# Later half gather and shorter router, reordered joint and last attention, products released by each turned column group

## The chip, the cores and the metric

The kernel runs on one core of a Trainium2 chip. The metric is the device time of one execution, in microseconds (us). The core's engines are TensorE (PE, matrix products and turns), VectorE (DVE), ScalarE (ACT), GpSimd (POOL) and SyncE (SP, which here only issues loads). Each engine runs its own instruction queue in order; semaphores tie the queues together, and 16 DMA engines move data. Everything is float32.

## The reference

One token block of 256 latent rows and two contexts of 256 rows, width 1024, goes through three layers. `first_block` is gated linear attention and a mixture of experts; `second_block` is a joint attention layer (latent attention with 8 heads and grouped attention with 8 heads over context and latent keys) and a last layer (windowed attention and a short convolution).

```python
# experts
scores = sigmoid(h @ w_router); sel = scores + b_router
# the best group of 4 of 16 experts by the sum of its best two, then its best two experts
out += gates[:, e] * ((silu(h @ w1[e]) * (h @ w3[e])) @ w2[e])      # every e
# joint layer
q, k, v = heads_ab(adaln(x, mod) @ w_in)                            # also for the context
x = x + gate * ((attention over [context, latent] * silu(g)) @ w_out)
xc = xc + gate_c * ((attention over context * silu(gc)) @ w_out)
# last layer
oc = window attention with sink; od = gb * short_conv(gcv * gh, conv_w)
x = x + gate * ((concat[oc, od] * silu(g)) @ w_out)
```

## The kernel before, in words

Each engine has one block of code, and the order of the calls in it is the order of its queue. There is no planner: all orders are written by hand, and the same list of steps stands in the blocks of PE, ACT and DVE.

**Banks.** `Banks` hands the eight accumulator banks out in turn. `open` makes PE wait until the eighth-last bank was evicted, `filled` tells the reader that it may evict, `wait` is that reader's wait.

**Turns and products.** `turn(use, src)` transposes normed rows with PE, eight column groups k into eight banks. ACT evicts the even groups (L1190), DVE the odd ones (L1706), with the modulation applied. `wait_turned(use)` then holds PE until all eight are there, and `project` (L562) or `project_T` (L574) runs eight products, one per k. Uses 0, 1, 3, 4 and 5 turn the first norm, the router's input, the latent rows of the joint layer, and the context and latent rows of the last layer.

**Router and gather.** The logits come from 16 small products on the turned rows (L746). DVE ranks the experts with linked small operations (L1882 to L1940): `places` (five operations) is called for each of the two token tiles, twice. PE counts tokens ahead (five products, L758 to L762), DVE makes the selection matrix `sel` (L1928, L1929), and PE gathers the tokens into expert order as products with `sel`, in two parts of 32 products (L771), which ACT (L1332) and DVE (L1944) evict.

**Experts.** 16 experts, one after another: GpSimd copies (`stage`, L2271) the 64 rows of an expert, PE runs `up` (32 products, L787), ACT takes Silu (L1377), DVE the product (L1974), PE turns it (L793), ACT copies it (L1379), PE runs `down` (16 products, L800). An expert with more than 64 tokens repeats this behind a branch. SP loads three pieces of 2 MB per expert into seven slots, in a fixed order (L1105); a slot of an `up` piece is free when that `up` is done, a `down` slot when that `down` is done. ACT and DVE run a hardware loop over eight pairs of experts.

**Joint layer.** Projections per tile, then queries and keys (L562, L899), grouped and latent norms on DVE that ask ACT for reciprocal roots (`head_rstd`, L1420 to L1423), turns of the heads (L908, L922), products for the gates (L849), then attention in 32 iterations of two units: turns of probabilities (L949), values (L958), scores three iterations ahead (L939). `ab_between` puts the modulation products of later layers (L530) between. `gate(u)` spreads a gate row over all partitions: DVE makes a diagonal (L1713), PE two products of four steps (L593), ACT two copies. Gates 2 and 3 come after the attention, then the eight output products (L562).

**Last layer.** Keys, values, queries, attention gates, output gates in two halves (`cdga`, L574), turns (L1051, L1055), then eight iterations of attention with twelve chunks of the convolution's input products (L574, two after each of the first six iterations), then the output.

## Time and profile before

| what | value |
| --- | --- |
| median of 3 runs | 1092.01 us (1090.19 to 1094.64) |
| the profiled execution, its own time | 1090.92 us |
| its span, first to last instruction | 1089.2 us |
| busy in the span | PE 969.7 us (89%), DVE 369.5 (34%), ACT 292.0 (27%), POOL 27.8 (3%) |
| mean granted TensorE clock | 0.969 of full |
| DMA traffic | 217.62 MB, mean 200 GB/s |

A busy PE is not PE at its peak, and a share over the whole span mixes stages with different limits. The rows below are read stage by stage: the instruction, when it started, how long it ran, and in brackets how long its engine had been idle before it and what released it.

### The profile page before, as it was taken

Reading aid. Unit: us, or ns where it says so; the run is one execution under the profiler, and the core shown is the slowest. Engines: PE = TensorE matmul, PEld = TensorE weight load, DVE = VectorE, ACT = ScalarE, POOL = GpSimd, SP = SyncE. Lnnn points to the kernel's source line nnn. Section 1 sums busy time; section 2 is a strip of 40 time slices with the busy share of each in tenths; the row PEclk is TensorE's granted clock in tenths of the full one; section 3 lists DMA queues with packets and bytes.
Section 4 is the critical chain, followed back from the end, with each engine's and each line's share of the span. In section 5 each row is a group of like instructions: output and inputs, shape, how many; then the busy total and the mean of one; then the engine's idle time right before and its main releaser. Section 6 shows DMA issues by size and latency. Waiting matters only on the chain.

```text
span 1089.2 us, 12096 instructions
## 1 busy us (share of the span) xinstructions
PE 969.7 (89%) x4358; PEld 518.8 (48%) x4359; DVE 369.5 (34%) x878; ACT 292.0 (27%) x678; POOL 27.8 (3%) x48
## 2 busy tenths in 40 slices
PE   3899989999878877688779999979999899997998
PEld 1464446554463322233225665557455445575763
DVE  1100597614540000000002231277667323246442
ACT  3210544233210000000001321356666211215320
POOL 0100200000000000000001000000000000000000
PEclk8999999999979989999989999989999999998999
DMA  9964565593597999989998202104644104332321
GB/s 352 320 230 156 103 232 194 177 335 106 193 348 287 398 395 397 397 339 398 394 397 301 78 1 78 68 1 155 225 139 102 40 0 149 102 136 78 94 62 39
DMA packets 99364, 217.62 MB, mean 200 GB/s; under 512 B 2853, under 2 KB 5209, under 8 KB 99177
## 3 DMA queue, kind: packets, MB, share of 16 engines
q1 hardware_dynamic: 94480, 206.45, 52.7%
q0 software_dynamic: 1696, 5.72, 2.1%
q10 hardware_dynamic: 3128, 4.62, 1.1%
q8 instruction: 42, 0.69, 0.3%
q14 instruction: 18, 0.14, 0.0%
HBM read 211.27 MB, written 5.51 MB: 199 GB/s over the span
## 4 chain that ended last, share of the span: by engine, by line
PE 74%; DMA 9%; DVE 6%; ACT 5%; issue 3%; SPq 2%; POOLq 0%; ACTq 0%; DVEq 0%; POOL 0%
PE bank L562 27%; PE bank L787 9%; PE bank L574 9%; DMA arena<-in_w_gate_e_dram 4%; PE bank L854 4%; PE bank L939 3%; PE bank L800 3%; PE bank L958 3%; DMA arena<-in_w_mod_dram 3%; PE bank L530 3%; PE bank L949 3%; DMA arena<-in_w_up_e_dram 2%; PE bank L771 2%; SPq L1105 1%; PE bank L849 1%
## 5 line engine op out<-in xcount | busy, mean ns | idle before, releaser
L562 PE MATMUL bank<-arena 128*128 128x512 f32 (+3 forms) x768 | 305.7, 556 | 4.0 <-ACT arena L1190 2.0
L562 PEld LDWEIGHTS bank<-arena 128*128 128x128 f32 x768 | 144.1, 190 | 153.6 <-issue 140.2
L787 PE MATMUL bank<-arena 128*64 128x512 f32 x544 | 130.8, 636 | 23.2 <-issue 23.2
L574 PE MATMUL bank<-arena 128*128 128x256 f32 (+1 forms) x384 | 99.3, 418 | 2.9 <-ACT arena L1539 1.5
L787 PEld LDWEIGHTS bank<-arena 128*64 128x64 f32 x544 | 46.2, 147 | 105.9 <-issue 105.9
L574 PEld LDWEIGHTS bank<-arena 128*128 128x128 f32 x384 | 72.5, 191 | 31.2 <-issue 21.7
L800 PE MATMUL bank<-arena 128*64 128x512 f32 x272 | 63.8, 610 | 9.6 <-ACT arena L1379 9.0
L1377 ACT ACTIVATE arena<-bank 128x256 f32<-128x256 f32 x16 | 6.1, 383 | 199.4 <-PE bank L787 199.4
L530 PE MATMUL bank<-arena,silu_c 128*32 128x512 f32 x384 | 50.2, 648 | 5.3 <-DMA arena<-in_w_mod_dram 2.9
L1974 DVE TENSOR_TENSOR arena<-arena,bank 128x256 f32<-128x256 f32 x16 | 6.7, 421 | 138.3 <-ACT arena L1377 138.3
L939 PE MATMUL bank<-arena 64*128 64x512 f32 (+3 forms) x160 | 49.6, 574 | 4.5 <-ACT arena L1636 2.3
L1539 ACT ACTIVATE arena<-bank,small 128x512 f32<-128x512 f32 (+1 forms) x80 | 47.9, 616 | 0.5
L1550 ACT ACTIVATE arena<-bank 128x512 f32<-128x512 f32 (+1 forms) x80 | 37.4, 516 | 20.0 <-PE bank L949 19.0
L949 PE MATMUL bank<-con,arena 128*128 128x128 f32 x256 | 37.8, 279 | 5.3 <-DVE arena L2139 3.4
L854 PE MATMUL bank<-arena 128*64 128x256 f32 x384 | 42.1, 380 | 0.0
L800 PEld LDWEIGHTS bank<-arena 128*64 128x64 f32 x272 | 21.9, 139 | 40.5 <-issue 40.5
L1723 DVE TENSOR_TENSOR arena<-bank,gate_rows 128x512 f32<-128x512 f32 x16 | 11.1, 692 | 88.4 <-PE bank L562 79.7
L949 PEld LDWEIGHTS bank<-con,arena 128*128 128x128 f32 x256 | 28.7, 141 | 22.4 <-DVE arena L2139 13.9
L2119 DVE TENSOR_REDUCE small<-bank 128x1 f32<-128x256 f32 (+1 forms) x64 | 33.9, 554 | 14.9 <-PE bank L939 14.4
L1977 DVE TENSOR_TENSOR gate_rows<-bank,gate_rows 128x512 f32<-128x512 f32 x16 | 11.1, 692 | 78.5 <-PE bank L800 78.5
L2139 DVE TENSOR_SCALAR arena<-arena,small 128x512 f32<-128x512 f32 (+1 forms) x80 | 34.7, 433 | 2.8
L854 PEld LDWEIGHTS bank<-arena 128*64 128x64 f32 x384 | 27.3, 137 | 15.7 <-issue 2.3
(327 smaller groups left out, 956.2 us busy)
## 6 DMA issues: line engine op xcount, KB each, us to landing
arena<-in_w_up_e_dram SPq DMA_DIRECT2D x16, 2048.0 KB, 20.3
arena<-in_w_gate_e_dram SPq DMA_DIRECT2D x16, 2048.0 KB, 20.0
arena<-in_w_down_e_dram SPq DMA_DIRECT2D x16, 2048.0 KB, 20.2
arena<-in_w_mod_dram SPq DMA_DIRECT2D x12, 2048.0 KB, 12.2
arena<-in_mod_w_dram SPq DMA_DIRECT2D x12, 2048.0 KB, 8.1
arena<-in_gla_w_in_dram SPq DMA_DIRECT2D x6, 2048.0 KB, 11.4
arena<-in_cd_w_in_dram SPq DMA_DIRECT2D x6, 2048.0 KB, 7.9
arena<-in_ab_w_in_dram SPq DMA_DIRECT2D x5, 2048.0 KB, 8.0
```

Of the source, the lines that this page charges most:

```text
L530: mm = pe.matmul(ps[32 * j:32 * j + 32, :], silu_c[:, blk, k, :], w[:, k, :], start=(k < 4), stop=(k >= 4), tile_position=(0, 32 * j))
L562: mm = pe.matmul(ps[:, 0:n], lhs[:, k, tile * P:(tile + 1) * P], w[:, k, c0:c0 + n], start=(k == 0), stop=(k == kd_ - 1))
L574: mm = pe.matmul(ps[:, i * n:(i + 1) * n], w[:, k, c * P:(c + 1) * P], rhs[:, k, 0:n], start=(k == 0), stop=(k == KC - 1))
L787: mm = pe.matmul(up_b[64 * j:64 * j + 64, :], h[:, k, :], blocks[:, g + n:u + n + 1:u - g, :], start=(k == 0), stop=(k == KC - 1), tile_po ...
L800: mm = pe.matmul(dn_b[64 * q:64 * q + 64, :], ffT[:, kc % 2, 64 * (kc // 2):64 * (kc // 2) + 64], w2[:, kc, 512 * q:512 * q + 512], start= ...
L854: mm = pe.matmul(ps[GD * v:GD * v + GD, n * T:(n + 1) * T], w[:, k, at:at + GD], rhs[:, k, 0:T], start=(k == 0), stop=(k == KC - 1), tile_ ...
L939: mm = pe.matmul(ps[:, 0:(hi - lo) * P], q, k, start=True, stop=True)
L949: mm = pe.transpose(ps[:, i * P:(i + 1) * P], prob[u % 4][:, i * P:(i + 1) * P], ident)
L1539: act.activation(prob[u % 4][:, 0:(hi - lo) * P], ps[:, 0:(hi - lo) * P], ACT.Exp, bias=per_unit(at_max, u), accum_out=per_unit(at_den, u) ...
L1550: act.activation(probT[g % 2][:, j, 0:hi - lo, P * (t % 2):P * (t % 2) + P], ps[:, 0:(hi - lo) * P].rearrange("p (k t) -> p k t", t=P), AC ...
L2119: dve.tensor_reduce(per_unit(at_max, u), ps[:, 0:(hi - lo) * P], AX.X, ALU.max, negate=True)\
L2139: dve.tensor_scalar(p, p, rden, None, ALU.mult).then_inc(p_scaled, 1)
```

## The change

Banks are handed out from a list, so that three can be held by the experts while the others turn over. `wait_turned` takes a column group and stands in the product's loop. The router ranks both tiles in one call, counts with two products, and writes `sel` part by part. The gather's second part stands behind expert 0's `up` on PE, and ahead of expert 0's Silu and product on ACT and DVE. ACT's and DVE's loops over experts are written out. GpSimd's handling of extra tokens stands behind the next copy; for expert 0 it stands ahead of expert 1's copy. In the joint layer two calls of `grouped_rstd` move ahead on ACT, gates 2 and 3 go into iterations 16 and 20, the flush to 28, and the first output product to 30; the wait for the last mixed groups stands before the fifth output product. In the last layer the second half of the output gates follows the turns of the keys, ACT's table load follows it, and one chunk of the convolution stands before the first iteration. Buffers move to constants that are no longer read.

```diff
     def open(self, pe, name, sem, value):
-        n = len(self.freed)
-        if n >= 8:
-            pe.wait_ge(*self.freed[n - 8])
-        self.freed.append((sem, value))
-        self.at[name] = n
-        return self.banks[n % 8]
+        n = self.order.pop(0)
+        if self.freed[n] is not None:
+            pe.wait_ge(*self.freed[n])
+        self.freed[n] = (sem, value)
+        self.used[n] += 1
+        self.at[name] = (n, self.used[n])
+        self.order.append(n)
+        return self.banks[n]
+
+    def hold(self, names):
+        self.held = [self.at[x][0] for x in names]
+        self.order = [n for n in self.order if n not in self.held]
+
+    def give_back(self):
+        self.order += self.held
 
...
-        act1, act2 = view(10240, 256), view(10496, 256)
-        ffT = view(10752, 2, P)
+        spent = con[:, cols["levels"][0]:cols["levels"][0] + 768]
+        act1, act2, ffT = spent[:, 0:256], spent[:, 256:512], spent[:, 512:768].rearrange("p (c s) -> p c s", c=2)
         y_buf = [gate_rows[:, 0, 0:512], gate_rows[:, 0, 512:1024]]
-        y_x, hs_x = view(11008, 512), view(SPARE + SLOT, KC, CAP)
+        y_x, hs_x = iota, gate_rows[:, 1, 512:1024].rearrange("p (k s) -> p k s", k=KC)
...
+        AB_GATE_AT, AB_OUT_AT = [16, 20], [30]
         CONV_CHUNKS = [(w, c) for w in ("cd3", "cd4", "cd2") for c in range(4)]
+        CONV_AT = [[0], [1, 2], [3, 4], [5, 6], [7, 8], [9, 10], [11], [], []]
...
-            def wait_turned(use):
-                pe.wait_ge(turned_a, 4 * TURN_AT[use] + 4)
-                pe.wait_ge(turned_v, 4 * TURN_AT[use] + 4)
-
-            def project(name, wname, c0, n, tile, lhs, sem_, value):
+            def wait_turned(use, k):
+
+                pe.wait_ge((turned_a, turned_v)[k % 2], 4 * TURN_AT[use] + k // 2 + 1)
+
+            def project(name, wname, c0, n, tile, lhs, sem_, value, turned=None):
...
                 for k in range(kd_):
+                    if turned is not None:
+                        wait_turned(turned, k)
                     mm = pe.matmul(ps[:, 0:n], lhs[:, k, tile * P:(tile + 1) * P], w[:, k, c0:c0 + n],
...
+                        if turned is not None and i == 0:
+                            wait_turned(turned, k)
...
             turn(0, xn)
-            wait_turned(0)
             for h in range(HG):
-                project_T(f"k{h}", "k", [h], 512, hT, k_ready, h + 1)
+                project_T(f"k{h}", "k", [h], 512, hT, k_ready, h + 1, turned=0 if h == 0 else None)
...
-            wait_turned(1)
             pe.wait_ge(route_in, 16)
             ps = banks.open(pe, "parts", parts_copied, 4)
             for k in range(KC):
                 j = k % 4
+                wait_turned(1, k)
                 mm = pe.matmul(ps[32 * j:32 * j + NE, 0:T], w_route[:, k, :], h2T[:, k, :],
...
             mask = small[:, 96:128].rearrange("p (t e) -> p t e", t=TT)
             ps = banks.open(pe, "ranks", ranked, 1)
-            pe.matmul(ps[:, 0:NE], before, mask[:, 0, :], start=True, stop=True)
-            pe.matmul(ps[:, NE:2 * NE], ones, mask[:, 0, :], start=True, stop=False)
-            pe.matmul(ps[:, NE:2 * NE], before, mask[:, 1, :], start=False, stop=True)
-            pe.matmul(ps[:, 2 * NE:3 * NE], ones, mask[:, 0, :], start=True, stop=False)
-            mm = pe.matmul(ps[:, 2 * NE:3 * NE], ones, mask[:, 1, :], start=False, stop=True)
+            both = mask.rearrange("p t e -> p (t e)")
+            pe.matmul(ps[:, 0:TT * NE], before, both, start=True, stop=True)
+            mm = pe.matmul(ps[:, TT * NE:2 * TT * NE], ones, both, start=True, stop=True)
...
-            pe.wait_ge(sel_ready, TT)
-            for part in range(2):
+            def gather(part):
+                pe.wait_ge(sel_ready, TT * (part + 1))
...
+            gather(0)
+
 
             moe = [banks.open(pe, f"moe{i}", experts_done, 1) for i in range(3)]
             up_b, t_b, dn_b = moe
+            banks.hold([f"moe{i}" for i in range(3)])
...
                 up(hs[e % 2], e, up_done)
+                if e == 0:
+                    gather(1)
                 pe.wait_ge(ff_ready, e + 1)
                 turn_ff(ff_turned)
...
-                wait_turned(use)
                 lhs, off = (hT_ctx, 2) if use == 2 else (hT_lat, 0)
                 for t in order:
-                    project(f"c{t}", "ab0", 0, 512, t - off, lhs, c_ready, AB_AT[t] + 1)
+                    project(f"c{t}", "ab0", 0, 512, t - off, lhs, c_ready, AB_AT[t] + 1,
+                            turned=use if t == order[0] else None)
...
-                if m == 30:
+                if m in AB_GATE_AT:
+                    gate(2 + AB_GATE_AT.index(m))
+                if m == 28:
                     mod_flush()
+                if m in AB_OUT_AT:
+                    pe.wait_ge(mixed, NG // 2)
+                    out_rows(AB_OUT_AT.index(m))
+
+            def out_rows(n):
+                t, c = ABY[n]
+                project(f"aby{c}{t}", f"abo{c}", 0, 512, t, mixT4, y_added, 4 + n + 1)
...
-            gate(2)
-            gate(3)
-            pe.wait_ge(mixed, NG)
             def keys_and_values(t):
-                project(f"cdkv{t}", "cd1", 0, 256, t, hT, cdkv_ready, CD_AT[t] + 1)
-
-            for n, (t, c) in enumerate(ABY):
-                project(f"aby{c}{t}", f"abo{c}", 0, 512, t, mixT4, y_added, 4 + n + 1)
+                project(f"cdkv{t}", "cd1", 0, 256, t, hT, cdkv_ready, CD_AT[t] + 1,
+                        turned=4 if t == 2 else 5 if t == 0 else None)
+
+            for n in range(len(AB_OUT_AT), len(ABY)):
+                if n == 4:
+                    pe.wait_ge(mixed, NG)
+                out_rows(n)
                 if n == 5:
                     turn(4, view(HIGH, 4, D))
-            wait_turned(4)
             for t in (2, 3):
                 keys_and_values(t)
             turn(5, view(HIGH, 4, D))
-            wait_turned(5)
...
-            for g in range(2):
-                project_T(f"cdga{g}", "cd6", [2 * g, 2 * g + 1], T, hT, cdga_ready, g + 1)
+            project_T("cdga0", "cd6", [0, 1], T, hT, cdga_ready, 1)
...
                 mm = pe.transpose(ps[:, t * P:(t + 1) * P], ckv_sb[:, t, 0:P], ident)
             banks.filled("wkT", mm)
+            project_T("cdga1", "cd6", [2, 3], T, hT, cdga_ready, 2)
             pe.wait_ge(gqkT_ready, 11)
...
             def cd_between(m):
-                for n in (2 * m, 2 * m + 1):
-                    if n < len(CONV_CHUNKS):
-                        w, c = CONV_CHUNKS[n]
-                        project_T(f"conv{n}", w, [c], T, hT, conv_in, n + 1)
+                for n in CONV_AT[m + 1]:
+                    w, c = CONV_CHUNKS[n]
+                    project_T(f"conv{n}", w, [c], T, hT, conv_in, n + 1)
 
             begin, run = attention(CD_GROUPS, NU, cd_probT, cd_scores, cd_values, lambda n: None, cd_between)
             begin()
+            cd_between(-1)
             run()
...
+            flags = extra_flag[0:1, :, :].rearrange("p e t -> p (e t)")
+            for e in range(NE):
+                i, b = e // 2, e % 2
+                act.wait_ge(hs_ready, e + 1)
+                slot0 = slot_of(act, e * (1 + EXTRA))
+                any_extra = act.value_load(flags[:, e * EXTRA:e * EXTRA + 1], min_val=0, max_val=1)
...
+                if e == 0:
+                    gather(1)
+                act.wait_ge(up_done, e + 1)
+                act.activation(act1, up_b[:, 0:256], ACT.Silu).then_inc(silu_done, 1)
...
+                if m in AB_GATE_AT:
+                    gate(2 + AB_GATE_AT.index(m))
 
             begin, run = attention(AB_GROUPS, 0, ab_probT, ab_between, False)
+            grouped_rstd(2)
             queries(0)
             keys_values(0)
-            grouped_rstd(2)
             queries(1)
...
             queries(2)
+            grouped_rstd(3)
             keys_values(2)
-            grouped_rstd(3)
...
-            gate(2)
-            gate(3)
...
-            for g in range(2):
+            def out_gates(g):
...
-            act.preload_act_table_set(LN_EXP)
+
+            out_gates(0)
             for t in range(TT):
                 ps = banks.wait(act, f"wqT{t}")
                 act.activation(qwT[:, :, t * P:(t + 1) * P], ps[:, :].rearrange("p (g t) -> p g t", g=4), ACT.Copy)\
                    .then_inc(gqkT_ready, 1)
             ps = banks.wait(act, "wkT")
             act.activation(kwT[:, :], ps[:, :], ACT.Copy).then_inc(gqkT_ready, 1)
+            out_gates(1)
+            act.preload_act_table_set(LN_EXP)
...
-            for t in range(TT):
-                places(place[:, t, :], pick[:, t, :], GROUPS, EPG)
+            places(place.rearrange("p t e -> p (t e)"), pick.rearrange("p t e -> p (t e)"), TT * GROUPS, EPG)
             link(dve.tensor_scalar(mask, place, 2.0, None, ALU.is_lt))
             link(dve.tensor_tensor(tmp32, pick, mask, ALU.mult))
             link(dve.tensor_reduce(gscore.rearrange("p t g -> p (t g)"),
                                    tmp32.rearrange("p t (g e) -> p (t g) e", e=EPG), AX.X, ALU.add))
-            for t in range(TT):
-                places(gplace[:, t, :], gscore[:, t, :], 1, GROUPS)
+            places(gplace.rearrange("p t g -> p (t g)"), gscore.rearrange("p t g -> p (t g)"), TT, GROUPS)
...
-            dve.tensor_copy(cnt, ps[:, 2 * NE:3 * NE])
-            dve.tensor_copy(rank, ps[:, 0:2 * NE].rearrange("p (t e) -> p t e", t=TT)).then_inc(ranked, 1)
+            ahead, all_ = (ps[:, i * TT * NE:(i + 1) * TT * NE].rearrange("p (t e) -> p t e", t=TT) for i in range(2))
+            dve.tensor_copy(rank, all_)
+            link(dve.tensor_copy(slot_v, ahead))
+            link(dve.tensor_tensor(cnt, rank[:, 0, :], rank[:, 1, :], ALU.add))
+            dve.tensor_tensor(slot_v[:, 1, :], slot_v[:, 1, :], rank[:, 0, :], ALU.add).then_inc(ranked, 1)
             dve.wait_ge(ranked, 1)
             link(dve.tensor_tensor_scan(slot0, ones[:, 0:NE], cnt, 0.0, ALU.mult, ALU.add))
             link(dve.tensor_tensor(slot0, slot0, cnt, ALU.subtract))
-            link(dve.tensor_tensor(slot_v, rank, outer(slot0, TT), ALU.add))
...
-            for t in range(TT):
-                link(dve.tensor_scalar(sel[:, t, :], iota, slots_ab[:, t, 0:1], None, ALU.is_equal))
-                dve.scalar_tensor_tensor(sel[:, t, :], iota, slots_ab[:, t, 1:2], sel[:, t, :], ALU.is_equal, ALU.add)\
-                   .then_inc(sel_ready, 1)
+            for part in range(2):
+                for t in range(TT):
+                    places_in, row = iota[:, T * part:T * part + T], sel[:, t, T * part:T * part + T]
+                    link(dve.tensor_scalar(row, places_in, slots_ab[:, t, 0:1], None, ALU.is_equal))
+                    dve.scalar_tensor_tensor(row, places_in, slots_ab[:, t, 1:2], row, ALU.is_equal, ALU.add)\
+                       .then_inc(sel_ready, 1)
...
-            for part in range(2):
+            def gather(part):
                 for k in range(1, KC, 2):
                     ps = banks.wait(dve, f"gath{part}{k}")
                     dve.tensor_scalar(hg[:, k, T * part:T * part + T], ps[:, 0:T], coef[:, 2, 0, k:k + 1],
                                       coef[:, 2, 1, k:k + 1], ALU.mult, ALU.add).then_inc(hg_v, 1)
-            up_b, t_b, dn_b = [banks.banks[banks.at[f"moe{i}"] % 8] for i in range(3)]
+
+            gather(0)
+            up_b, t_b, dn_b = [banks.banks[banks.at[f"moe{i}"][0]] for i in range(3)]
             dve.wait_ge(gate_bc, 4)
 
...
-                if m == 30:
+                if m + 1 in AB_GATE_AT:
+                    gate(2 + AB_GATE_AT.index(m + 1), mod2[:, 0, 16:24, AB_GATE_AT.index(m + 1)])
+                if m == 28:
                     mod_col(23)
...
-            gate(2, mod2[:, 0, 16:24, 0])
-            gate(3, mod2[:, 0, 16:24, 1])
...
             stage(0, 0)
+            stage_extra(0)
             pool.wait_ge(hg_a, KC)
             pool.wait_ge(hg_v, KC)
             stage(1, 1)
...
             with pool.Fori(0, NE // 2 - 1) as i:
                 for b in range(2):
                     e = i * 2 + b
-                    stage_extra(e)
                     pool.wait_ge(up_done, e + 1)
                     stage(e + 2, b)
-            stage_extra(NE - 2)
-            pool.wait_ge(up_done, NE - 1)
+                    stage_extra(e + 1)
             stage_extra(NE - 1)
...
```

## Rows read from the trace of the kernel before

**Rows 1.** The page: GB/s of 40 slices, and the ended-last chain by engine.

```profile
GB/s 352 320 230 156 103 232 194 177 335 106 193 348 287 398 395 397 397 339 398 394 397 301 78 1 78 68 1 155 225 139 102 40 0 149 102 136 78 94 62 39
...
PE 74%; DMA 9%; DVE 6%; ACT 5%; issue 3%; SPq 2%; POOLq 0%; ACTq 0%; DVEq 0%; POOL 0%
```

**Rows 2.** Chain in order of time: start us, us, what.

```profile
372.99 20.42 DMA arena<-in_w_up_e_dram
```

**Rows 3.** Timeline, router: start us, us, engine, line, instruction [idle before <-releaser].

```profile
292.84 1.06 PE L746 MATMUL bank<-arena,w_route 128*16 128x256 f32 x16 [1.42 <-ACT arena L1190]
...
297.02 0.22 DVE L1892 TENSOR_TENSOR small<-small 128x64 f32<-128x64 f32 x1
...
302.32 0.61 PE L758 MATMUL bank<-small,con 128*128 128x16 f32 x2 [4.20 <-DVE small L1908]
...
304.74 0.17 DVE L1915 COPY small<-bank 128x16 f32<-128x16 f32 x1 [1.60 <-PE bank L762]
...
306.56 0.49 DVE L1928 TENSOR_SCALAR arena<-con,small 128x512 f32<-128x512 f32 x1
```

**Rows 4.** Timeline, gather, expert 0 and expert 1's down.

```profile
309.07 17.09 PE L771 MATMUL bank<-arena 128*128 128x256 f32 x64 [4.44 <-DVE arena L1929]
...
319.30 0.54 DVE L1944 TENSOR_SCALAR arena<-bank,coef 128x256 f32<-128x256 f32 x1 [1.18 <-PE bank L771]
...
320.91 0.61 POOL L2271 COPY arena<-arena 128x512 f32 x1 [18.06 <-ACT arena L1332]
...
326.09 7.09 PE L787 MATMUL bank<-arena 128*64 128x512 f32 x32
...
335.57 5.35 PE L800 MATMUL bank<-arena 128*64 128x512 f32 x16 [0.56 <-ACT arena L1379]
...
349.80 3.65 PE L800 MATMUL bank<-arena 128*64 128x512 f32 x16 [0.56 <-ACT arena L1379]
```

**Rows 5.** Windows: stretch, busy us per engine, granted clock, DMA share, GB/s.

```profile
324.00:326.00 2.00, 2.00 (x11) 1.55 (x9) 0.54 (x1) 0.82 (x3) 0.00 (x0) 1.00 0.08 29
...
334.00:336.00 2.00, 0.87 (x4) 0.46 (x6) 0.42 (x1) 0.38 (x1) 0.61 (x1) 0.92 0.76 161
...
336.00:338.00 2.00, 2.00 (x6) 0.59 (x4) 0.00 (x0) 0.00 (x0) 0.00 (x0) 0.50 1.03 372
```

**Rows 6.** Timeline, first products behind turns 0, 3 and 5.

```profile
38.93 13.99 PE L574 MATMUL bank<-arena 128*128 128x512 f32 x32 [1.36 <-ACT arena L1190]
...
645.30 13.97 PE L562 MATMUL bank<-arena 128*128 128x512 f32 x32 [0.83 <-ACT arena L1190]
...
928.95 3.26 PE L562 MATMUL bank<-arena 128*128 128x256 f32 x14 [1.16 <-ACT arena L1190]
```

**Rows 7.** Timeline, heads of the joint attention.

```profile
703.39 0.69 DVE L2031 TENSOR_TENSOR mod_rows<-arena,rstd 128x512 f32<-128x512 f32 x1 [9.04 <-ACT rstd L1423]
...
714.65 3.55 PE L922 MATMUL bank<-con,arena 128*96 128x128 f32 x16 [5.76 <-DVE arena L2102]
...
725.83 0.69 DVE L2031 TENSOR_TENSOR mod_rows<-arena,rstd 128x512 f32<-128x512 f32 x1 [3.37 <-ACT rstd L1423]
...
745.63 1.91 PE L922 MATMUL bank<-con,arena 128*96 128x128 f32 x16
```

**Rows 8.** Timeline, end of the joint attention.

```profile
853.36 1.95 PE L958 MATMUL bank<-arena,gate_rows 128*64 128x256 f32 x16 [0.74 <-ACT arena L1550]
...
856.96 1.98 PE L593 MATMUL bank<-gate_diag,con 128*128 128x512 f32 x4 [1.66 <-DVE gate_diag L1713]
...
862.09 18.19 PE L562 MATMUL bank<-arena 128*128 128x512 f32 x42
```

**Rows 9.** Timeline, start of the last attention.

```profile
983.09 4.43 PE L939 MATMUL bank<-arena 64*128 64x512 f32 x12 [2.26 <-ACT arena L1636]
...
990.01 1.71 PE L949 MATMUL bank<-con,arena 128*128 128x128 f32 x8 [2.49 <-DVE arena L2139]
```

**Rows 10.** Waits of PE, experts: engine, line, releaser: us in total, times, longest.

```profile
PE bank L787 <- issue: 23.2, 9, 3.8
```

167 lines of the change are left out of this document (82 added, 85 removed).

## The prediction

> **What bounds the kernel now.** Read the page's shares of the chain that ended last first, then the GB/s of its 40 slices: TensorE (PE) carries 74% of the chain and DMA 9%, and for eight of nine slices in the middle the traffic stands at 394 to 398 GB/s [rows 1]. So there are two regimes. Outside the experts a piece of PE time, or PE idle that is not itself a wait for a load, is worth its length. Inside the experts the chain runs through expert weights, for example 20.42 us on one load [rows 2]; there only what brings the first buffers back earlier counts. Then read the timeline at each edited place for the idle ahead of the first PE instruction and its releaser.
>
> **Products behind a turning wait (turns 0, 3 and 5).** PE waited 1.36, 0.83 and 1.16 us for the last of eight turned column groups [rows 6]. Now group k releases only product k, and ScalarE and VectorE finish the eight groups in pairs. Turn 0: PE is free at 38.93 - 1.36 = 37.57, where about four groups are ready, and a product of 32/4 = 8 steps takes 13.99/4 = 3.5 us, so it ends at 41.1 instead of 42.4: 1.3 us. Its bounds are 0 (the weights of k may land only then; no row shows it) and 1.36. Turn 3: the same arithmetic gives 0.8. Turn 5: eight 256-column steps take about 1.8 us (3.26 us for 14, [rows 6]), and the last group ends them at one step after 928.9; 929.1 instead of 930.7 is 1.5, bounds 0.5 and 1.6. What waits behind these waits on PE is only the same product, so a wait costs nothing else.
>
> **Router.** The logits' first product waited 1.42 us for turn 1 and took 1.06 [rows 3]; run along with the evictions it ends one step after the last: 0.9 us less. From the first ranking comparison at 297.02 to the first rank product at 302.32 VectorE runs 25 linked operations, 0.21 us each [rows 3]. Batching both tiles removes 10 (2.1), doubled widths of the ten left cost back some 0.4 in all: 1.7. Five rank products become two; they took from 302.32 to the copy at 304.74, about 0.43 each, so 1.3 less, and two more linked operations behind them give 0.4 back. The first selection now writes half the width: 306.56 to the gather's start at 309.07 is 2.5 us; full and half price of the elements bound it by 2.5 and 1.25, I take 1.7, so 0.8. Together 3.4, with turn 1 about 4.2 us.
>
> **Gather in halves.** The whole gather is 64 products in 17.09 us. Its first half ended about 319.2 (its last eviction starts at 319.30), GpSimd copied expert 0's rows at 320.91 for 0.61, and up(0) could not start before 326.09 because the second half stood in PE's queue [rows 4]. Now up(0) starts 0.1 after the copy, at 321.6: 4.5 earlier, and with the router 8.7 earlier, 317.4. It ends at t0 = 324.5. But the second half (about 6.9 us at full clock: 326.1 - 319.2) is now between up(0) and down(0), and the 2.4 us chain of Silu, product, turn, copy (333.18 to 335.57, [rows 4]) is mostly still open behind it, since ScalarE and VectorE first evict the half.
>
> What does that do to the loads? DMA had nothing from about 324 (29 GB/s in 324:326) until the first returned buffers, issued at 333.2, moved data from about 334.5 [rows 5]; a 2.1 MB load at 395 GB/s [rows 1] takes 5.3 us. Before: two loads by up(0) fill 334.5 to 345.1, the third is released by down(0) at 335.57 + 5.35 = 340.9, the next two by up(1) 7 us later, and the queue is never empty; five loads are through at 361.0. After: two loads fill t0+1.3 to t0+11.9; down(0) ends at t0 + 6.9 + 2.3 + 3.65 = t0+12.9 (3.65 is down(1) at full clock, [rows 4]), so the third load moves only from t0+14.2 to t0+19.5, and the two by up(1) from t0+21.1 to t0+31.7 = 356.2. The loads are 4.8 us ahead of 361.0: of 8.7 us earlier start, 3.9 are given back in two new holes. One price more: the clock. In the 2.4 us gap before down(0) the granted clock fell to its 1.2 GHz level (0.92 in 334:336, 0.50 in 336:338), and down(0) took 5.35 instead of 3.65 [rows 4, 5]. The new gap ahead of up(0) is as long and has no matrix work in it at all; I charge 1.7 once. Experts: 4.8 - 1.7 = 3.1 us. Bounds: both gaps slow and PE's half of the gather late, -1; no fall, +4.8. The loads carry this shift to the end of the experts, since from 373 on PE waits for them by far more [rows 2].
>
> The Trainium skill (TensorE: Matmul & The Clock Gate, Part 4: PE-mode transpose) says that transposes don't count as busy for that clock. The drop in a gap that contained two transposes agrees with it; by that rule the gap after the second half, which has only transposes in it, would cost another 1.7, and the total below would be 1069.4.
>
> **Unrolled loops, banks, other queues.** ScalarE's and VectorE's loop over pairs of experts goes; its registers and branches lay beside up (7.09 us): 0, but see D. Three banks are held from the first half on, so the second half turns over five; each is evicted 0.5 us after it is filled: 0. GpSimd stages expert 1 about 2.3 us after the second half ends, wanted 5.8 after: 0. SP's load of cd2 now waits for the moved gate half, 1.7 us later, and is used more than 20 us after it lands: 0.
>
> **Heads of the joint attention.** VectorE idled 9.04 us until 703.39 and 3.37 until 725.83 for reciprocal roots whose sums were ready: ScalarE had queries and keys ahead of them in its queue [rows 7]. Moved ahead, the first three small activations (0.8 us) run while ScalarE had waited anyway; VectorE's grouped norm then runs from 697.2 to 702.5, inside the old idle, and the latent norm starts at 702.8 (the copies it needs end there) rather than 708.7. Its result reaches PE at 709.5, not 714.65, behind PE's own work until 708.9: of 5.76 us idle 0.6 stay, and the 16 transposes take 1.9 as the later ones (745.63) instead of 3.55 [rows 7]. That is 5.1 + 1.6 = 6.7. Next late would be the second latent norm, wanted at 717.4 and due at 715.4, then nothing: 14 us of gate products follow and PE reaches the transposes of 745.63 at 738.9. Bounds 3 (ScalarE's order makes the second norm late) and 7.
>
> **Joint attention.** Its last values ended at 853.36 + 1.95 = 855.3 and the output products began at 862.09: 6.8 us of two gate rounds on the path [rows 8]. They go into iterations 16 and 20, where PE is busy almost without a hole, so their products stay as a cost: 2 x 1.98 = 4.0 [rows 8]. VectorE's diagonal and ScalarE's copies lie under PE there, bounds 0 and 1.5 more. The first output product moves forward ahead of the last turns, and the three others stand in front of the wait for the last mixed group, which covers it. The small flush moves by two iterations at no price. 6.8 - 4.0 = 2.8; take 2.9 for half-filled holes, bounds 1 and 3.5.
>
> **Last attention.** Before: PE waited 2.26 us for the evicted keys, ran the first scores in 4.43 us, waited 2.49, and at the slow clock its next steps were long too [rows 9]. The second half of the output gates (7 us) now stands between the turns and the scores and covers the 2.26, paid back by nothing since it only moves; the first conv chunk (3.5) stands in the 2.49. At full clock the three scores take 3.3, and turns, scores and convs after them lose about 2 us of slowness. 2.3 + 1.1 + 2.5 + 2.0 = 7.9, less 1.0 for what ScalarE evicts later (the gate half and its table load now run beside the first scores): 6.9. The tail keeps its waits, as only one chunk stands in iteration 5 but two iterations of exponentials are done by then. Bounds 3 and 8.
>
> **Sum.** 1.3 + 3.1 + 0.8 + 6.7 + 2.9 + 1.5 + 6.9 = 23.2 us off the profiled execution's own 1090.92 (span 1089.2 and 1.7 around it): 1067.7. The median of the runs shown is 1.1 above that execution, which would give 1068.8. Forecast 1068.
>
> **The rivals.**
> *A, queues, not PE, hold the two reordered stages.* For: ScalarE and VectorE have in-order chains there and the estimates leave 2 us. Against: in the trace both idle for PE. Heads 3, last attention 3: 1068 + 7.6 = 1076. Chance 0.2.
> *B, the early up(0) gives the experts nothing:* the holes at the third and fourth load eat it, with two slow gaps: 1068 + 4 = 1072. For: 3.9 us of it are already in my sum. Chance 0.12.
> *C, the change doesn't do what it says at the turns:* weights or the second evicting engine arrive last. 1068 + 1.3 + 0.9 + 0.8 + 1.5 = 1072.5. Chance 0.06.
> *D, slower: code.* Straight code for 16 experts is fetched anew for each on ScalarE and VectorE while the queues are full. PE, straight already, shows 23.2 us in 9 waits put down to issue, up to 3.8 [rows 10], though those hold waits for loads as well. If each engine lost 3 us between up and down of each expert, 6.0 against the 3.8 that PE waits at most would be 2.2 x 16 = 35 us more: 1103. It decides from 5.3 us per expert on (3.8 + 24/16). Against: the code after a wait has 7 us of up to arrive. Chance 0.04.
> The Trainium skill (Runtime: NRT & Kernel Launch, Instruction fetch mechanics) gives D its reason: fetching ahead is sequential, and a taken branch out of its window has to fetch first; every expert skips the body for extra tokens. No run here shows such a fetch on these two engines.
> *Forecast:* 0.58, its own range 1063 to 1073.
>
> **Range and chances.** 1061 to 1079 holds the forecast, A, B and C. What a measurement of this kernel can tell from no change is about 0.5%, 5.5 us. Faster 0.94, same 0.02, slower 0.04.
>
> **What would show it.** Right: PE idle before the first latent transposes under 1 us; gates inside the attention and no hole between the last values and output product 4 of over 1 us; scores of the last attention released by PE's own queue, not ScalarE; up(0) starting some 9 us earlier relative to the transposes of turn 1; a DMA hole of 2 us after the second returned load; total traffic rate unchanged behind it. Wrong: expert 15's last product ending later than about 574 (before 577.8, less 1.3 and 3.1), idle on PE named after ScalarE in the heads, gate rounds costing over 2 us each, or Silu starting later than 0.5 us behind up.

## The result and the profile after

The changed kernel takes 1066.45 us (median of 4 runs, 1066.13 to 1070.58), the kernel before 1093.33 us (4 runs, 1090.19 to 1097.04). The ratio is 0.9762 with a 95% interval of 0.9736 to 0.9788. The forecast was 1068 us. The profiled execution took 1066.23 us with a span of 1064.5, against 1090.92 and 1089.2 before: 24.7 us, where the sum said 23.2.

From the page of the changed kernel, the lines that answer to [rows 1]:

```profile
GB/s 352 335 235 160 79 263 158 182 301 188 96 395 339 400 394 398 394 339 394 397 396 352 128 1 79 70 1 158 165 153 146 14 40 82 156 159 79 116 44 39
...
PE 77%; DMA 9%; DVE 5%; ACT 3%; issue 2%; SPq 2%; POOLq 1%; ACTq 0%; POOL 0%; DVEq 0%
```

The rate in the middle is the old one, 394 to 400 GB/s but for two slices at 339 (before: 394 to 398, with one such slice among eight). On PE 15.1 us of idle time went, and 9.6 us of busy time (969.7 to 960.1), as less of it ran at the slow clock (mean granted clock 0.978, before 0.969); the other engines' share of the chain fell, so PE's rose. Laid out by stage, with the same instruction as the mark in both chains of waits:

| stage, mark at its end | before, us | after, us | gain | predicted |
|---|---|---|---|---|
| start to the norm after the first attention's output | 284.02 | 284.12 | -0.1 | 1.3 |
| router and experts, to the first product of the joint layer | 294.39 | 288.87 | 5.5 | 3.1 |
| to the first product behind turn 3 | 66.89 | 66.07 | 0.8 | 0.8 |
| heads, to iteration 2's first scores | 114.65 | 107.36 | 7.3 | 6.7 |
| joint attention, to the second output product | 109.02 | 106.59 | 2.4 | 2.9 |
| turns 4 and 5, to the gates of the last layer | 80.86 | 79.51 | 1.4 | 1.5 |
| last attention, to its first output product | 107.65 | 100.27 | 7.4 | 6.9 |

**Turn 0.** The timeline of PE at the second pair of value products, and windows of the same place (columns as in [rows 5]):

```profile
110.17 15.70 PE L578 MATMUL bank<-arena 128*128 128x512 f32 x32
```

```profile
110.00:112.00 2.00, 2.00 (x5) 0.96 (x4) 2.00 (x4) 0.00 (x0) 1.42 (x2) 0.65 0.00 0
112.00:114.00 2.00, 2.00 (x3) 0.66 (x2) 1.06 (x2) 1.57 (x1) 2.00 (x5) 0.50 0.59 96
```

The products that came 1.45 us earlier (37.48 in the chain, against 38.93 in [rows 6]) were followed by a pair that took 15.7 us instead of 14.0, with PE busy all the time and its granted clock at 0.50, the 1.2 GHz level. Before it, PE had run 3.7 us of products with 16 rows. The profile of the kernel before shows no fall there.

**Router, gather, expert 0.** The timeline that answers to [rows 3, 4]:

```profile
291.46 2.04 PE L763 MATMUL bank<-arena,w_route 128*16 128x256 f32 x16
...
296.42 0.29 DVE L1927 TENSOR_TENSOR small<-small 128x128 f32<-128x128 f32 x1
...
300.03 0.64 PE L776 MATMUL bank<-small,con 128*128 128x32 f32 x2 [3.22 <-DVE small L1941]
...
303.44 0.35 DVE L1966 TENSOR_SCALAR arena<-con,small 128x256 f32<-128x256 f32 x1
...
305.16 8.85 PE L786 MATMUL bank<-arena 128*128 128x256 f32 x32 [4.07 <-DVE arena L1967]
...
315.67 0.61 POOL L2311 COPY arena<-arena 128x512 f32 x1 [15.11 <-issue]
...
316.33 7.09 PE L805 MATMUL bank<-arena 128*64 128x512 f32 x32 [2.33 <-POOL arena L2311]
...
323.35 7.17 PE L786 MATMUL bank<-arena 128*128 128x256 f32 x32
```

The wait for turn 1 is gone, the ranking takes 3.6 us (296.42 to 300.03) where it took 5.3, and the gather starts at 305.16 instead of 309.07. up(0) comes 9.8 us earlier, at full clock, after a gap of 2.33 us. Down(0) runs at 332.49 in 3.65 us, not in the 5.35 of [rows 4]. Of the two holes that the prediction laid out in the loads, the first shows as two windows at half the rate; windows of 1 us, GB/s last:

```profile
336.00:337.00 1.00, 1.00 (x8) 0.47 (x6) 0.69 (x1) 0.00 (x0) 0.00 (x0) 1.00 1.06 410
337.00:338.00 1.00, 1.00 (x7) 0.34 (x4) 0.00 (x0) 0.00 (x0) 0.00 (x0) 1.00 0.82 176
338.00:339.00 1.00, 1.00 (x8) 0.39 (x6) 0.00 (x0) 0.00 (x0) 0.00 (x0) 1.00 0.57 195
```

The second, expected near 344, is no hole: the windows from 339 to 343 moved 293 to 338 GB/s, those of 343 to 345 over 400 and the next 305.

**Later stages.** Timelines of the changed kernel's PE against [rows 7 to 9]: the first latent transposes and the two gate rounds inside the joint attention; then the product behind the last values, the last attention's first scores and the step behind the convolution chunk.

```profile
702.77 1.95 PE L943 MATMUL bank<-con,arena 128*96 128x128 f32 x16 [0.37 <-DVE arena L2142]
...
787.96 1.88 PE L611 MATMUL bank<-gate_diag,con 128*128 128x512 f32 x4
...
807.09 1.88 PE L611 MATMUL bank<-gate_diag,con 128*128 128x512 f32 x4
...
852.94 9.28 PE L578 MATMUL bank<-arena 128*128 128x512 f32 x21
...
963.45 2.85 PE L960 MATMUL bank<-arena 64*128 64x512 f32 x12
966.23 3.72 PE L592 MATMUL bank<-arena 128*128 128x256 f32 x16
970.37 1.44 PE L970 MATMUL bank<-con,arena 128*128 128x128 f32 x8 [0.42 <-DVE arena L2179]
```

A wait of 5.76 us became 0.37, the output products start on the heels of the last values, the waits of 2.26 and 2.49 us became none and 0.42, and the slow clock of [rows 9] (three scores in 4.43 us, now 2.85) did not come.

### The profile page after: what moved, and what is told of

It reads as the page before. It is cut to its first block, busy times and chain, and to the rows that moved or that the text cites. A ratio compares the mean times of both kernels' runs of the same rounds, so it can differ in the third digit from the quotient of the medians.

```text
span 1064.5 us, 11944 instructions
## 1 busy us (share of the span) xinstructions
PE 960.1 (90%) x4352; PEld 513.7 (48%) x4353; DVE 368.5 (35%) x874; ACT 291.8 (27%) x678; POOL 27.8 (3%) x48
## 4 chain that ended last, share of the span: by engine, by line
PE 77%; DMA 9%; DVE 5%; ACT 3%; issue 2%; SPq 2%; POOLq 1%; ACTq 0%; POOL 0%; DVEq 0%
PE bank L578 27%; PE bank L805 9%; PE bank L592 9%; DMA arena<-in_w_up_e_dram 4%; PE bank L875 4%; PE bank L818 3%; PE bank L960 3%; PE bank L979 3%; PE bank L544 3%; PE bank L870 3%; PE bank L970 3%; DMA arena<-in_w_gate_e_dram 2%; DMA arena<-in_w_mod_dram 2%; SPq L1133 2%; PE bank L786 2%
## 5 line engine op out<-in xcount | busy, mean ns | idle before, releaser
L578 PEld LDWEIGHTS bank<-arena 128*128 128x128 f32 x768 | 144.4, 191 | 152.0 <-issue 140.8
L805 PE MATMUL bank<-arena 128*64 128x512 f32 x512 | 122.0, 631 | 22.6 <-issue 20.3
L805 PEld LDWEIGHTS bank<-arena 128*64 128x64 f32 x512 | 43.8, 145 | 98.9 <-issue 96.1
L818 PE MATMUL bank<-arena,con 128*64 128x512 f32 x272 | 62.1, 597 | 9.6 <-ACT con L1409 9.0
L1407 ACT ACTIVATE con<-bank 128x256 f32<-128x256 f32 x16 | 6.1, 383 | 191.3 <-PE bank L805 191.3
L2014 DVE TENSOR_TENSOR con<-con,bank 128x256 f32<-128x256 f32 x16 | 6.7, 421 | 131.1 <-ACT con L1407 131.1
L960 PE MATMUL bank<-arena 64*128 64x512 f32 (+3 forms) x160 | 47.1, 540 | 2.2 <-ACT arena L1569 2.2
L818 PEld LDWEIGHTS bank<-arena,con 128*64 128x64 f32 x272 | 21.5, 136 | 39.3 <-issue 39.3
L875 PEld LDWEIGHTS bank<-arena 128*64 128x64 f32 x384 | 27.3, 137 | 15.7 <-issue 2.3
L1758 DVE TENSOR_TENSOR arena<-bank,gate_rows 128x512 f32<-128x512 f32 x12 | 8.3, 692 | 63.5 <-PE bank L578 63.5
```

Of the source, the lines that this page charges most:

```text
L578: mm = pe.matmul(ps[:, 0:n], lhs[:, k, tile * P:(tile + 1) * P], w[:, k, c0:c0 + n], start=(k == 0), stop=(k == kd_ - 1))
L805: mm = pe.matmul(up_b[64 * j:64 * j + 64, :], h[:, k, :], blocks[:, g + n:u + n + 1:u - g, :], start=(k == 0), stop=(k == KC - 1), tile_po ...
L818: mm = pe.matmul(dn_b[64 * q:64 * q + 64, :], ffT[:, kc % 2, 64 * (kc // 2):64 * (kc // 2) + 64], w2[:, kc, 512 * q:512 * q + 512], start= ...
L875: mm = pe.matmul(ps[GD * v:GD * v + GD, n * T:(n + 1) * T], w[:, k, at:at + GD], rhs[:, k, 0:T], start=(k == 0), stop=(k == KC - 1), tile_ ...
L960: mm = pe.matmul(ps[:, 0:(hi - lo) * P], q, k, start=True, stop=True)
```

## The experiments

Each time is a median; each ratio is to the kernel before, run on the same chip. The times of one kernel differ by up to 10 us from one execution to the next, so the verdicts on parts rest on the stages of the traces, the ratios beside them.

**1. Turn 0 alone.** Kernel before, with:

```diff
-            wait_turned(0)
+                        if turned is not None and i == 0:
+                            pe.wait_ge((turned_a, turned_v)[k % 2], 4 * TURN_AT[turned] + k // 2 + 1)
```

> Kernel before with one edit: the first key product waits for each turned column group by itself. In the changed kernel the products started 1.45 us earlier, but the second pair of value products (110.2 to 125.9) took 15.7 us instead of 14.0 with a granted clock of 0.65 and 0.50 between 110 and 114, where the kernel before had 1.00, although PE never stood idle. Theory (clock): the same fall comes again, since nothing ahead of it differs from the changed kernel; value product 3 ends at 125.8 to 125.9, the stage is not shorter, and the whole time is that of before within 0.5 us. Rival (something else held PE there, such as an eviction that the other parts of the change moved): no fall, value product 3 ends at 124.3, and the whole is 1.3 to 1.5 us faster by the trace's span.

Measured: 1091.63 against 1092.35 us, ratio 0.9983 (0.9963 to 1.0003). The fall came again (0.83, 0.50 and 0.81 in the three windows from 110 to 116). That looked like the theory, but runs 2 and 3, whose text up to there is that of the kernel before, have it too. Windows of run 2, with turn 0 as it was:

```profile
110.00:112.00 2.00, 2.00 (x11) 0.72 (x8) 2.00 (x5) 0.00 (x0) 0.00 (x0) 0.92 0.00 0
112.00:114.00 2.00, 2.00 (x3) 0.97 (x4) 2.00 (x5) 0.00 (x0) 1.79 (x3) 0.50 0.10 12
```

So the fall is not caused by the change, and the reason given in the expectation was wrong: the same text ahead of the place doesn't decide whether it comes. Run 9 put this to the test.

**2. Heads alone.** Kernel before, with ScalarE's order:

```diff
+            grouped_rstd(2)
             queries(0)
             keys_values(0)
-            grouped_rstd(2)
@@
             queries(2)
+            grouped_rstd(3)
             keys_values(2)
-            grouped_rstd(3)
```

> Kernel before with one edit: ScalarE takes the reciprocal roots of the grouped queries ahead of the queries and keys that stood in its queue. Theory: this alone gives what the heads' stage gained in the changed kernel, 7.3 us (first latent transpose 5.1 us earlier and at full clock, no granted clock of 0.5 around 712): ratio 0.9933, span 1082. The trace must show VectorE's waits of 9.04 and 3.37 us gone. Rival (the stage gained because PE arrived in it in another state, or from the banks' new order): under 3 us, ratio 0.997 or more.

Measured: 1084.00 us, ratio 0.9914 (0.9886 to 0.9942), which holds 0.9933. In the profile the first latent transposes have lost their wait, exactly as in the changed kernel:

```profile
710.36 1.95 PE L922 MATMUL bank<-con,arena 128*96 128x128 f32 x16 [0.38 <-DVE arena L2102]
```

The stage itself is 3.9 us shorter in this execution, the slowest of the five (1088.57), not 7: a fall came at 750 to 757 instead of the old one at 710 to 716.

**3. Joint attention alone.** Kernel before, with:

```diff
+                if m in AB_GATE_AT:
+                    gate(2 + AB_GATE_AT.index(m))
+                if m in AB_OUT_AT:
+                    pe.wait_ge(mixed, NG // 2)
+                    out_rows(AB_OUT_AT.index(m))
@@
-            gate(2)
-            gate(3)
-            pe.wait_ge(mixed, NG)
```

> Kernel before with the joint attention's part alone: the two rows of gates are built in iterations 16 and 20, the first output product runs in iteration 30, the small flush in iteration 28. Theory: 2.4 us, as in the changed kernel (6.8 us of gate rounds leave the path, some 3.5 to 4 us of their products and the longer iterations stay): ratio 0.9978. Rival (the gates' products fall into holes that PE had there anyway): 6 us, ratio 0.9945. A second rival (exponentials are late by the two gates' copies on ScalarE): nothing, ratio 1.000.

Measured: 1089.63 us, ratio 0.9974 (0.9952 to 0.9995). From the start of modulation product 18 to the last layer's gates it needs 186.01 us against 188.72: 2.7. The theory holds, both rivals fall.

**4. Last attention alone.** Kernel before, with the split output gates and one convolution chunk ahead of the first iteration (the rest of the change's part as it stands in the diff):

```diff
+            project_T("cdga1", "cd6", [2, 3], T, hT, cdga_ready, 2)
             pe.wait_ge(gqkT_ready, 11)
@@
             begin()
+            cd_between(-1)
             run()
```

> Kernel before with the last attention's part alone: second half of the output gates behind the turns, one convolution chunk ahead of the first iteration, table load behind both. Theory: the 7.4 us of the changed kernel come from here alone: ratio 0.9932, and no granted clock under 1.00 between 980 and 1000. Rival (half of it came from the earlier arrival of turns 4 and 5 and of the joint attention's evictions): 3 to 4 us, ratio 0.9965.

Measured: 1083.86 us, ratio 0.9908 (0.9874 to 0.9941). From the gates to the first output product 100.45 us, before 107.82, changed kernel 100.44. No clock under 1.00 in the stage. All of it comes from here.

**5 and 6. Both halves first, and that with loops.** Changed kernel, with

```diff
             gather(0)
+            gather(1)
@@
                 up(hs[e % 2], e, up_done)
-                if e == 0:
-                    gather(1)
```

and the same on ScalarE and VectorE; in 6 these two run their loop over eight pairs again.

> Changed kernel with one part undone: both halves of the gather run ahead of up(0) again; the shorter router and everything else stay. Theory (two holes in the loads): starting up(0) some 4.5 us earlier is given back almost whole, because the third load waits for down(0), which stands behind the second half, and the fourth and fifth wait for up(1); so undoing it costs only about 0.6 to 1.2 us from the last gate rows before the router to the end of expert 15. Rival (the early up(0) is worth its length): 4 to 4.5 us more, whole kernel 0.4% slower than the changed one.

> As both_halves_first, and ScalarE and VectorE run their loop over eight pairs of experts as in the kernel before, in place of straight code for 16 experts. Theory (code is free, as the instructions between two experts have 7 us of up to arrive): expert stage equal to both_halves_first within 0.3 us. Rival D (straight code is fetched anew for every expert): with loops the stage is shorter by 1 us or more, and Silu starts sooner behind up than with straight code.

Measured: 1070.48 us, ratio 0.9794 (0.9743 to 0.9846), and 1070.75 us, 0.9792 (0.9738 to 0.9845). From turn 1's last group of transposes to the start of expert 15's down it takes 279.18 and 279.42 us; in the changed kernel 279.58. The early up(0) is worth nothing that these profiles show, and they speak against the rival's 4 us. They don't exclude it: the distance varies from 278.2 to 284.0 us over four profiles of the changed kernel's text (run 10), run 5's profiled execution was the fastest of its five (1064.87), and the whole times, 0.9794 and 0.9792 against 0.9762, lie 0.3% higher (against run 9's 0.9778 0.15%), where the rival named 0.4%, within intervals of half a per cent either way. Straight code costs nothing that shows: 0.24 us between 5 and 6, the same wait of 1.02 us between up(0) and the turn behind it in both, and PE's waits in the experts no longer with it than with loops. Waits of PE in the stage, changed kernel first, loops second (as [rows 10]; run 5: 22.5 us in 8 waits):

```profile
PE bank L805 <- issue: 23.1, 9, 4.1
```

```profile
PE bank L806 <- issue: 26.3, 10, 4.4
```

**7. Whole waits.** Changed kernel, where the first product behind each turn waits for groups 7 and 8 (`if k == 0: wait_turned(turned, 6); wait_turned(turned, 7)`).

> Changed kernel with the turning waits whole again (turns 0, 1, 3, 4 and 5: the first product waits for all eight column groups). Theory: turn 0 1.4, the router's first product 0.9, turn 3 0.8 and turn 5 1.4 us come back, in all 4.5 us of PE time, of which turn 0's part can hide under a fall of the granted clock at 110: 3.1 to 4.5 us over the changed kernel, ratio to before 0.979 to 0.981. Rival (the order of the first products' steps doesn't matter, since the evictions end when they end and PE only waits inside the product): under 1 us.

Measured: 1071.57 us, ratio 0.9799 (0.9748 to 0.9851). The waits are back, at turns 0, 1, 3 and 5:

```profile
39.41 2.81 PE L594 MATMUL bank<-arena 128*128 128x512 f32 x6 [1.57 <-ACT arena L1222]
...
293.39 1.06 PE L767 MATMUL bank<-arena,w_route 128*16 128x256 f32 x16 [1.46 <-DVE arena L1744]
...
642.84 3.67 PE L579 MATMUL bank<-arena 128*128 128x512 f32 x8 [0.88 <-DVE arena L1744]
...
916.77 18.73 PE L579 MATMUL bank<-arena 128*128 128x256 f32 x59 [0.85 <-DVE arena L1744]
```

Their sum is 4.76 us, and the profiled execution (1071.37) is 5.1 us over the changed kernel's, in which turn 0's gain was lost to the clock while here up(0) ran with a fall. The mechanism is shown; its total only within such falls.

**8. No chunk ahead.** Changed kernel with `CONV_AT = [[], [0, 1], [2, 3], [4, 5], [6, 7], [8, 9], [10, 11], [], []]`.

> Changed kernel with the last attention's convolution chunks one iteration later: none ahead of the first iteration, two in each of the next six; the split output gates stay. Theory: the chunk ahead of the first iteration covered the wait of 2.49 us for the exponentials (and kept the clock up), so the last attention takes 2 to 3.5 us more than in the changed kernel. Rival (the gate half alone did it): within 0.5 us of the changed kernel.

Measured: 1075.09 us, ratio 0.983 (0.9779 to 0.9881). The stage takes 105.27 us, 4.8 more than in the changed kernel; the wait is back, and behind it a granted clock of 0.50 in 972:974:

```profile
971.03 1.90 PE L970 MATMUL bank<-con,arena 128*128 128x128 f32 x8 [4.07 <-DVE arena L2179]
```

The theory's sign is right, its 2 to 3.5 us too low. Of the 7.4 us the one chunk ahead of the first iteration carries 4.8; the other 2.6 are, by difference, the gate half's.

**9. The changed kernel once more.**

> The changed kernel once more, unedited, beside its own variants. Theory (the falls of the granted clock are drawn anew in each execution and not set by the kernel's text): the stage times without a fall repeat within 0.1 us (heads 107.3, last attention 100.4, turn 3 and turn 5 as before), while the falls at 110, around 320, at 405 to 460 and at 742 come at other places or not at all, and shift the end by 1.5 to 3 us. Rival (they belong to the kernel): the profile repeats with a fall at 110 to 114 and none before up(0) or at 742. Ratio to before 0.976 in either case.

Measured: 1067.07 us, ratio 0.9778 (0.9754 to 0.9801). The profile is another one. The value products and a window that had 0.50:

```profile
110.19 14.00 PE L578 MATMUL bank<-arena 128*128 128x512 f32 x32
```

```profile
112.00:114.00 2.00, 2.00 (x6) 0.95 (x5) 1.07 (x2) 1.55 (x1) 2.00 (x5) 1.00 0.59 92
```

Turn 0's lead is kept this time: turn 1's last transposes start at 287.46, against 289.27 in the first profile and 289.17 before. Instead up(0) ran slowly behind its 2.33 us gap:

```profile
316.00:318.00 2.00, 2.00 (x6) 0.48 (x4) 0.00 (x0) 0.00 (x0) 0.00 (x0) 0.52 1.02 386
318.00:320.00 2.00, 2.00 (x8) 0.62 (x6) 0.00 (x0) 0.00 (x0) 0.00 (x0) 0.62 1.05 387
```

It took 8.78 us for 7.09, the 1.7 that the prediction charged; the gather's first half, behind a wait of 4.06 us, came back to full clock later and took 10.08 us for 8.85; and the heads had a fall at 742 to 747 (1.5 us). The theory holds for these places, and the last attention repeats to 0.01 us (100.44). It doesn't hold for all: the four ups between 404 and 465, each behind a wait of 2 to 3.3 us, took 8.5 to 8.8 us in both profiles. Over all 14 profiles of this study the fall near 110 came 7 times, in kernels with either form of turn 0.

**10. Direct up(0).** Changed kernel, with

```diff
-                pe.wait_ge(hs_ready, e + 1)
-                up(hs[e % 2], e, up_done)
                 if e == 0:
+                    up(hg[:, :, 0:CAP], e, up_done, direct=True)
                     gather(1)
+                else:
+                    pe.wait_ge(hs_ready, e + 1)
+                    up(hs[e % 2], e, up_done)
@@
-            stage(0, 0)
+            pool.sem_inc(hs_ready, 1)
```

> Changed kernel; expert 0's first rows begin at place 0 always, so up(0) reads the gathered columns where they lie, each step released by the eviction of its column group, and GpSimd's copy for expert 0 is gone. Theory (loads wait for the buffers that up(0), down(0) and up(1) return, and all three move with up(0)): the wait of 2.33 us before up(0) goes, up(0) starts 2.2 us earlier and the loads and the expert stage with it; 2 us less up to the doubled expert's first up, where the changed kernel stood 151.8 us behind the last gate rows' product: 149.8. Rival (a lead of the loads is lost as that of the split gather seemed to be): the start is earlier and the end of the stage is not.

Measured: 1066.43 us (1061.47 to 1069.51), ratio 0.9772 (0.9753 to 0.9791). Timeline of PE, with the gap gone:

```profile
303.19 8.95 PE L786 MATMUL bank<-arena 128*128 128x256 f32 x32 [4.07 <-DVE arena L1971]
312.06 7.09 PE L807 MATMUL bank<-arena 128*64 128x512 f32 x32
```

The doubled expert's first up stands 149.4 us behind the last gate rows' product (run 12: 150.8), where 149.8 was expected. From turn 1's last transposes to expert 15's down it takes 275.28 us, and 277.04 in run 12. The same distance with this stage's text of before is 284.98, 283.09, 284.66, 287.04 and 284.37, with that of the changed kernel 279.58, 280.72, 278.21 and 284.04. Both with the direct up(0) are below every one without; by the means 4.5 us less than the changed kernel's text. That is more than the wait of 2.33 us; neither of the two had a slow up(0), which three of the five profiles with the wait had (below). The distance to the doubled expert parts the two causes: 151.8 and 152.0 us in the two profiles with the wait and a fast up(0) (first, run 8), 154.7 and 155.4 in two with a slow one (runs 9 and 11). Run 10, whose first half of the gather took 8.95 us as against their 8.85 to 8.87, is 2.4 to 2.6 us shorter, which is the wait; run 12 lost 1.0 in that half (9.92). The other 3 us go with the slow up(0) and a slower first half of the gather ahead of it (10.1 us). In the ratio this doesn't show: 0.9772 against 0.9778; and run 10's profiled execution was the fastest of its five (1061.47 against a median of 1066.43).

**11 and 12. Early sum, and both.** Changed kernel, VectorE:

```diff
-            for t in range(2, 4):
-                ps = banks.wait(dve, f"v0_{t}")
-                dve.tensor_copy(v_sb[:, t, 0:512], ps[:, :]).then_inc(v_ready, 1)
-            mod_col(6)
             for z in range(2):
+                ps = banks.wait(dve, f"v0_{2 + z}")
+                dve.tensor_copy(v_sb[:, 2 + z, 0:512], ps[:, :]).then_inc(v_ready, 1)
                 dve.wait_ge(softplus_ready, z + 1)
...
+            mod_col(6)
```

> Changed kernel; VectorE takes the first half of the softplus sum between value products 2 and 3, the second right behind value product 3, and the modulation column only then. Theory: between 126 and 155 the chain of the changed kernel runs through VectorE alone, so the scans start at 129.5 instead of 133.46 and the first level's products at 151.5 instead of 155.36; 3.5 to 4 us less to the end, and a clock fall at 110 then costs nothing. Rival (the load that PE waited for at 223.6, 8.2 us, ends when it ends): that wait grows by what was won and the total stays.

> Changed kernel with both edits, the direct up(0) and the early sum. Theory: they lie in stages behind one another and add: 5.5 to 6 us less than the changed kernel, ratio to before about 0.971. Rival: the router or the doubled expert takes one of the two back: 2 to 4 us.

Measured: 1070.01 us, ratio 0.9797 (0.9783 to 0.9811), and 1064.07 us, 0.9761 (0.9739 to 0.9782). The early sum did nothing: run 11 is 2.9 us above the changed kernel beside it, not 3.5 to 4 below. The first level's products start at 154.32 in run 12, against 153.84 in run 9 and 155.36 in the first profile. The chain of run 12, in order of time, shows what took over:

```profile
126.03 8.65 DMA arena<-in_w_mod_dram
134.72 1.93 PE bank L544 x16
136.65 0.59 PE bank L532 x4
137.24 6.88 PE bank L578 x16
```

The load of a modulation weight leads, which neither the theory nor the rival named. It leads in the chains of run 9 (8.09 us from 126.11) and of the kernel before (7.96 us from 127.80) as well. VectorE leads there in only three of the 14 chains: in the first profile of the changed kernel and in run 2, with a fall at 110, and in run 10, without one (from 127.03). In the other eleven a load leads, in five of them behind such a fall. The two paths end close together, so that shortening one gives nothing, and the theory was read off one execution in which the load's path happened to be the shorter. Run 12 has the lowest median of the study, 3.0 us under the changed kernel's run beside it, and the shorter expert stage; but the two intervals overlap, so the times alone don't prove it faster.

## Why the prediction was right

**The reading was right: PE's idle time outside the experts is worth its length.** Heads 7.3 (6.7 said), last attention 7.4 (6.9), joint 2.4 (2.9; alone 2.7), turns 3 and 5 2.2 (2.3). Runs 2, 3, 4 and 7 show each by itself, run 2 by its whole time only. The last attention and the joint attention repeat to 0.02 us in every profile with their whole new text; the heads' 7.3 is a draw without a fall. Of the nine profiles with this stage's new text six have a fall near 742 that takes 1.5 us back (46.2 us instead of 44.6 from the first latent transposes to the next modulation product), so the gain is 7.3 in three and 5.8 in six, and 6.7 lies between. In the heads the two terms were 5.1 and 1.6; 5.6 and 1.6 came (69.35 us from turn 3's product to the transposes, now 63.71, and 3.55 to 1.95). In the joint attention the gates cost 2 x 1.88 inside the iterations, where 2 x 1.98 had been taken from [rows 8].

**Last attention: sum right, parts off.** The working gave 2.3 to the gate half, 1.1 to the chunk, the rest to the clock. Run 8 gives the chunk 4.8: without it the wait is 4.07 us, not 2.49. The two agree: at the slow clock the scores of [rows 9] took 4.43 us and hid 1.58 more of the same chain on VectorE than the 2.85 us that they take now (2.49 + 1.58 = 4.07). What was booked as slowness of the scores was a wait in another form, and only the chunk removes both.

**Experts: 3.1 predicted, 5.5 in the profile.** The router's 4.2 came as 3.9 (309.07 to 305.16). The holes in the loads were mis-sized: up(0) came 9.9 us earlier counted from turn 1's last transposes, and at 150 us behind them the changed kernel had loaded 2.81 MB more (57.93 against 55.12), which is 7.1 us at 395 GB/s, where the working had 4.8; so 2.8 us were given back, not 3.9. For the split gather the working had left 0.6 us (4.8 of loads against 4.2 of router); at that point run 5's loads are 0.49 MB, 1.2 us, behind, and at the end of the stage runs 5 and 6 find nothing of it. The other term that was mis-sized is the clock: 1.7 was charged as certain; in the first profile it did not fall due, in run 9 it did. The last up, on the other hand, ran slowly in the first profile (8.45 us for 7.10), which took 1.35 of a lead of 6.8 us. Over all profiles with the stage's old and new text the gain is 4.2 us (means 284.8 and 280.6, from 283.1 to 287.0 in five and from 278.2 to 284.0 in four), so 3.1 is within what single profiles scatter.

**A step missing from the working: the doubled expert.** One expert has more than 64 tokens and runs twice. Around it PE, not DMA, is late: the next load waits for a buffer and the traffic nearly stops. Windows of the changed kernel, and the timeline of that expert's two ups:

```profile
462.00:464.00 2.00, 1.80 (x10) 0.34 (x6) 0.00 (x0) 0.15 (x1) 0.00 (x0) 1.00 0.19 71
464.00:466.00 2.00, 0.62 (x4) 0.41 (x6) 0.42 (x1) 0.61 (x2) 0.61 (x1) 1.00 0.41 53
```

```profile
438.04 8.78 PE L805 MATMUL bank<-arena,gate_rows 128*64 128x512 f32 x32 [2.85 <-issue]
...
455.01 8.78 PE L805 MATMUL bank<-arena 128*64 128x512 f32 x32 [2.60 <-issue]
```

The first of the two in run 5:

```profile
438.17 7.09 PE L806 MATMUL bank<-arena,gate_rows 128*64 128x512 f32 x32 [1.60 <-POOLq L2322]
```

Up to here the changed kernel's loads had been ahead of run 5's by 1.2 us (0.47 MB at equal distance from turn 1); in the next 10 us that lead was gone (0.27 MB behind), since that expert's first up ran at full clock in run 5 (7.09 us) and partly at half in the changed kernel (8.78). "The loads carry this shift to the end of the experts" was therefore wrong in form: they carry it to the doubled expert, and PE's own position carries it on.

**Turn 0: 1.3 predicted, -0.1 in the profile.** The step "products end 1.3 earlier" was right (1.45 at the start, 1.7 at 106). It was lost to a fall of the clock, and in run 9 it was not: 1.7 there. The term was right, its first reading in the trace misleading.

**The number.** That 24.7 came where 23.2 was said is partly luck. In the first profile turn 0's gain was lost to a fall (1.7 us), while up(0) and the heads escaped the falls that most profiles have there (1.7 and 1.5 us). The whole times hold the forecast even so: 1066.45 and, in run 9, 1067.07 us.

**The rivals.** A: refuted, both stages gave their whole sum. B: refuted as to the total (the stage gave 4.2 us by the means, with the router's 3.9 in them), right about the split gather as far as the profiles of runs 5 and 6 show. C: refuted by run 7. D: refuted by run 6, as its 35 us are far beyond the scatter.

The Trainium skill (Runtime: NRT & Kernel Launch, Instruction fetch mechanics) had given D its reason, that a taken branch out of the fetched window must fetch first. On ScalarE and VectorE these runs show no such price. The 2.60 us of "issue" on PE behind the doubled expert's extra body, in every profile, would fit it, but was not tested.

The prediction also priced what would follow if transposes don't count as busy (the Trainium skill, TensorE: Matmul & The Clock Gate, Part 4: PE-mode transpose): another 1.7 us in the gap after the gather's second half, which holds only transposes. None of the seven profiles with that gap of 1.97 us shows a fall there; down(0) took 3.65 us in each. The Trainium skill (TensorE: Matmul & The Clock Gate, Part 1: The HAM clock gate) says that activity is watched in a window that runs freely. That agrees with falls that come in one execution and not in the next at the same instruction, as the one near 110 did.

## What to carry to other kernels

Outside a load-bound stage, list PE's waits with their releaser and give each independent work that is already in the queue; a single chunk of 3.5 us at the right place was worth 4.8 here. Inside a load-bound stage an earlier start counts only if every buffer's return moves with it: moving the second half of the gather behind up(0) moved one return and delayed the next, while taking 2.3 us out ahead of all of them paid in full as far as the doubled expert (the whole times don't show it). And one profile of a kernel is one draw of the clock: before a stage that "gave back" 1.7 us is explained by the change, read the granted clock there and in a second profile of the same kernel.
